# Three quarters of a query projection by Strassen's seven products, in one layer of an encoder

## The chip, the cores and the metric

The kernel runs on one core of one Trainium2 chip. A core has a matrix engine (PE, with its weight loads shown apart as PEld), a vector engine (DVE), an activation engine (ACT), a general engine (POOL) that here mostly issues DMAs, and a queue processor (SP) that only issues DMAs. Each engine runs its own list of instructions in order; they wait for each other by semaphores. The metric is the device time of one execution in microseconds. A lower number is better.

## The reference, cut to what matters

One layer of a streaming encoder on 1024 prompt tokens and 64 decode tokens, model width 1024. The change touches the cross-attention queries and, by a wait, the memory projections.

```python
def memory_kv(mem, norm_mem, w_xk, w_xv, xk_norm):
    mn = rmsnorm(mem, norm_mem)
    mk = rmsnorm((mn @ w_xk).reshape(bsz, N_MEM, N_HEADS_X, HEAD_DIM_X), xk_norm)
    mv = (mn @ w_xv).reshape(bsz, N_MEM, N_HEADS_X, HEAD_DIM_X)
    return mk, mv

def cross_attention(xn, mk, mv, w_xq, xq_norm, w_xo):
    q = rmsnorm((xn @ w_xq).reshape(bsz, t, N_HEADS_X, HEAD_DIM_X), xq_norm)   # 4 heads of 256
    s = jnp.einsum('bqhd,bkhd->bhqk', q, mk).astype(jnp.float32) * (HEAD_DIM_X ** -0.5)
    p = jax.nn.softmax(s, axis=-1).astype(mv.dtype)
    o = jnp.einsum('bhqk,bkhd->bqhd', p, mv).reshape(bsz, t, N_HEADS_X * HEAD_DIM_X)
    return o @ w_xo

def sq_relu_mlp(xn, w_up, w_down):
    return jnp.square(jax.nn.relu(xn @ w_up)) @ w_down
```

## The kernel before

Activations stand transposed: 8 tiles `y(0)` to `y(7)` of 128 features by 1092 token columns (1088 used) in the buffer `Y`. A dense stage is a row of output tiles. For one output tile ("tile" below) a slab of 128x1024 weights is loaded into `RAW`, split by ACT into a high part and by DVE into a low part (`act_split`, `dve_split`), and PE does for each of 8 row blocks the three products high x high, high x low, low x high, each in three column pieces of 364, 364 and 360: 72 matmuls (`pe_part`, L431). The tile builds up in three banks of the eight banks of PE's accumulator memory `ps` and is read out by DVE.

The stages run in the order: memory keys and values (`mem_tile`, 16 tiles of 256 columns), input projection with its mixers, output projection, query projection, cross-attention loop, its output projection, up-projection, down-projection. The up-projection does two tiles densely and the other thirty as 15 pairs by a Strassen scheme: a pair of tiles is a 2x2 block of weights (two output tiles by two halves of the rows) times a 2x2 block of activations (two halves of the rows by two halves of the tokens), which needs 7 products in place of 8. One product is 4 row blocks x 3 terms x 2 pieces of 272 columns = 24 matmuls (`product`, L2950). The combinations of the activation blocks (`t_raw`, `t_hi`, `t_lo`) are made once at the stage's entry, while PE does the two dense tiles; sums of weight blocks (`left_sum`), their split (`left_hi` on ACT, `left_lo` on DVE), copies of products out of `ps` (`prod_copy` on ACT) and the adding up of output blocks (`combine` on DVE) go on beside the products.

The query projection before is eight dense tiles, two for each of four heads. After a head's two tiles its features are squared by ACT (`xq_sq`, L1374), PE adds the squares up (`pe_stat`, L472, 16 matmuls), ACT and DVE turn the sum into a reciprocal root in the row buffer `stat_mix`, PE broadcasts the row in two halves (`pe_bcast`, L484), and DVE scales the head by each half (`xq_nrm`, L2025). A second broadcast waits until DVE has used up the first (semaphore `bc_used`). For head 0 to 2 this stands inside the tiles of the next head, for head 3 inside the attention loop. Before the first head the same is done once for the norm of the input: that broadcast gives `rstd`.

The attention loop has 20 units `u` (5 for each head). For each, PE computes scores of 256 queries by 256 memory rows (`xscores`, L2784, three units ahead), DVE takes the extreme (`xmin`), ACT the exponential (`xexp`), DVE normalises (`xnorm`), PE transposes (`xtransposes`, L2797), ACT and DVE split the transposed weights (`xpt_copy`, `xpt_lo`), and every second unit PE multiplies by the values (`xvalues`, L2817). The values of a head are split at units 0, 1, 4, 11 (ACT L1419, DVE `v_lo`, L2090). Each engine's list is written out by hand; nothing reorders it.

## Time and profile before

| | us |
|---|---|
| time, median of 3 (lowest, highest) | 1517.52 (1516.76, 1517.57) |
| profiled execution: its own time | 1518.14 |
| profiled execution: span | 1516.4 |
| PE busy | 1501.0 |
| DVE busy | 973.0 |
| ACT busy | 585.0 |

The span is what the profiler's instructions cover; 1.7 us of the profiled execution lie around it. Positions below, such as "at 669.75", are microseconds from the start of that span.

### The profile page before, as it was taken

The numbers are of one execution on the slowest core, as the hardware profiler recorded it, in microseconds if no ns is written. First come the engines' busy times: TensorE is split into PE (matmuls) and PEld (weight loads), VectorE is DVE, ScalarE is ACT, GpSimd is POOL, SyncE is SP. The second block draws the span as 40 slices with busy tenths as digits, with TensorE's granted clock in tenths as the row PEclk, the third lists the DMA queues.
The fourth block names the chain that finished last, engine by engine and source line by source line (L and its number), as shares of the span: only waits on it lengthen the run. The fifth ranks groups of instructions, "written<-read, shape, count | busy, mean of one in ns | idle before, by whom it ended". The sixth has DMA issues, their size and how long they took to land.

```text
span 1516.4 us, 26684 instructions
## 1 busy us (share of the span) xinstructions
PE 1501.0 (99%) x10924; PEld 1449.1 (96%) x10924; DVE 973.0 (64%) x1373; ACT 585.0 (39%) x1001; POOL 244.0 (16%) x322
## 2 busy tenths in 40 slices
PE   9999999999999999999999999999999999999999
PEld 8999999988779999997999999999999999999999
DVE  7636787757788443457443986666666597547653
ACT  7521031146675221235323743333434343433332
POOL 1010000002100100000000064445544310010110
PEclk9999999999999999999999999999999999999999
DMA  8425111103112533022222253443345975454663
GB/s 281 144 102 174 54 42 42 46 1 95 70 37 80 167 128 127 15 71 89 71 87 80 79 188 130 160 152 140 136 160 188 322 232 181 120 177 123 187 211 103
DMA packets 64495, 189.33 MB, mean 125 GB/s; under 512 B 7936, under 2 KB 12344, under 8 KB 64240
## 3 DMA queue, kind: packets, MB, share of 16 engines
q1 hardware_dynamic: 39824, 95.30, 19.4%
q0 software_dynamic: 24560, 92.45, 16.9%
q8 instruction: 81, 1.33, 0.4%
q14 instruction: 30, 0.25, 0.1%
HBM read 138.58 MB, written 54.12 MB: 127 GB/s over the span
## 4 chain that ended last, share of the span: by engine, by line
PE 53%; DMA 2%; DVE 1%; issue 0%; ACT 0%; SPq 0%; DVEq 0%; ACTq 0%
PE ps L2950 21%; PE ps L2974 19%; PE ps L431 8%; DMA a<-wdn 2%; PE ps L2784 2%; PE ps L2817 2%; PE ps L2797 0%; DMA r_raw_a<-quads_d 0%; PE ps L2827 0%; DVE Y L2276 0%; PE ps L484 0%; DVE B_lo L2074 0%; PE ps L472 0%; DVE r_lo_a L2251 0%; DVE s L2234 0%
## 5 line engine op out<-in xcount | busy, mean ns | idle before, releaser
L431 PE MATMUL ps<-A_hi,w_hi 128*128 128x364 f32 (+1 forms) x768 | 171.2, 331 | 0.3 <-DVE Y L1640 0.3
L431 PE MATMUL ps<-A_lo,w_hi 128*128 128x364 f32 (+1 forms) x768 | 169.0, 328 | 0.0
L431 PE MATMUL ps<-A_hi,w_lo 128*128 128x364 f32 (+1 forms) x768 | 168.1, 327 | 0.0
L394 ACT ACTIVATE w_hi<-w_raw 128x1024 fp32r<-128x1024 f32 x42 | 44.2, 1058 | 285.8 <-PE ps L431 184.0
L431 PEld LDWEIGHTS ps<-A_hi,w_hi 128*128 128x128 f32 x768 | 130.7, 188 | 7.5 <-issue 6.9
L431 PEld LDWEIGHTS ps<-A_lo,w_hi 128*128 128x128 f32 x768 | 132.7, 188 | 0.0
L431 PEld LDWEIGHTS ps<-A_hi,w_lo 128*128 128x128 f32 x768 | 132.5, 188 | 0.0
L398 DVE TENSOR_TENSOR w_lo<-w_raw,w_hi 128x1024 fp32r<-128x1024 f32 x42 | 51.1, 1222 | 100.5 <-ACT w_hi L394 100.3
L2950 PE MATMUL ps<-t_hi,wq_hi 128*128 128x272 f32 x480 | 99.3, 288 | 0.3 <-issue 0.3
L2950 PE MATMUL ps<-t_lo,wq_hi 128*128 128x272 f32 x480 | 99.2, 288 | 0.0
L2950 PE MATMUL ps<-t_hi,wq_lo 128*128 128x272 f32 x480 | 99.1, 288 | 0.0
L2974 PE MATMUL ps<-r_lo_b,wq_hi 128*128 128x272 f32 x448 | 93.7, 290 | 0.0
L2974 PE MATMUL ps<-r_hi_b,wq_hi 128*128 128x272 f32 x448 | 93.5, 290 | 0.0
L2974 PE MATMUL ps<-r_hi_b,wq_lo 128*128 128x272 f32 x448 | 93.5, 289 | 0.0
L2974 PE MATMUL ps<-r_hi_a,wq_hi 128*128 128x272 f32 x448 | 92.8, 288 | 0.4 <-DVE r_lo_a L2251 0.4
L2974 PE MATMUL ps<-r_lo_a,wq_hi 128*128 128x272 f32 x448 | 92.7, 288 | 0.0
L2974 PE MATMUL ps<-r_hi_a,wq_lo 128*128 128x272 f32 x448 | 92.5, 287 | 0.0
L1700 DVE SCALAR_TENSOR_TENSOR conv_acc<-ua_ext,params,conv_acc 128x1118 f32<-128x1118 f32 x58 | 76.2, 1377 | 0.0
L2950 PEld LDWEIGHTS ps<-t_hi,wq_hi 128*128 128x128 f32 x480 | 75.2, 188 | 0.4 <-issue 0.4
L2950 PEld LDWEIGHTS ps<-t_lo,wq_hi 128*128 128x128 f32 x480 | 75.3, 188 | 0.0
L2950 PEld LDWEIGHTS ps<-t_hi,wq_lo 128*128 128x128 f32 x480 | 75.2, 188 | 0.0
L2950 PE MATMUL ps<-A_hi,wq_lo 128*128 128x272 f32 x360 | 74.5, 288 | 0.0
(334 smaller groups left out, 3560.5 us busy)
## 6 DMA issues: line engine op xcount, KB each, us to landing
w_raw<-slabs SPq DMA_DIRECT2D x67, 512.0 KB, 3.6
quads_d<-quad_sum POOLq DMA_DIRECT2D x64, 272.0 KB, 2.9
w_raw<-wdn POOLq DMA_DIRECT2D x32, 512.0 KB, 3.9
r_raw_a<-quads_d SPq DMA_DIRECT2D x56, 272.0 KB, 3.0
r_raw_b<-quads_d SPq DMA_DIRECT2D x56, 272.0 KB, 3.2
quads_d<-hid_stage POOLq DMA_DIRECT2D x48, 272.0 KB, 3.1
Y<-xT POOLq DMA_DIRECT2D x16, 546.0 KB, 4.9
y_d<-Y POOLq DMA_DIRECT2D x16, 546.0 KB, 3.1
```

What stands on the lines that cost most here:

```text
L394: e.activation(WH[:, par], RAW[:, par], ACT.Copy).then_inc(s.w_hi, 1)
L398: e.tensor_tensor(WL[:, par], RAW[:, par], WH[:, par].bitcast(F32), ALU.subtract).then_inc(s.w_lo, 1)
L431: ins = e.matmul(PS[:, 3 * par + c, 0:n_], wt[:, wpar, w], xt[:, col:col + n_], start=(first and n == 0 and m == 0), stop=(last and n == l ...
L1700: e.scalar_tensor_tensor(CAV[:, h], UE[:, h, j:j + CAW], w, CAV[:, h], ALU.mult, ALU.add)\
L2784: ins = e.matmul(PS[:, u % 3, b * NMEM:(b + 1) * NMEM], y(2 * h + k)[:, q0:q0 + P], XKV[h][:, kk, k * NMEM:(k + 1) * NMEM], start=(k == 0) ...
L2817: ins = e.matmul(PS[:, 6 + d, :], wt[:, h, v0:v0 + P], xt[turn][:, k, :], start=(m == 0 and k == 0), stop=(m == 2 and k == 1))
L2950: ins = e.matmul(PS[:, b + c, 0:HC], WQ[wx][:, n % 4, k * P:(k + 1) * P], right(i, xx, k, c), start=(i in (0, 1, 3) and k == 0 and m == 0) ...
L2974: ins = e.matmul(PS[:, 2 * g + c, 0:HC], WQ[wx][:, down_slot(n), g * P:(g + 1) * P], down_right(xx, n)[:, c * HC:(c + 1) * HC], start=(ii ...
```

## The change

Head 0 keeps its two dense tiles. Heads 1 to 3, six tiles, become three pairs of seven products, with the scheme of the up-projection (`q_product` for `product`, and so on). The block sums of the activations are made at the entry of the query stage in the free buffer `B`, and the blocks of results are put together in `Y`, which is free there once the input has been stored; the scale by `rstd` that was part of reading out a tile is now three extra DVE operations of 128x544 for each pair (`q_scale`) and part of the fourth combine. The squares, statistic, root and broadcasts of each head move: head 0's into the products of pair 1, head 1's into those of pair 2 (in banks 0 and 1), head 2's into the attention loop at units 0 to 2; head 3's stay at units 6 to 11, but their squares move from before the loop to unit 1. The root of heads 0 to 2 is by logarithm and exponential (as head 3's was), so the DVE reciprocal goes. The loads of the heads' keys and values move from the start of the query stage to its last products, since their place holds the activation sums. In the memory stage tiles 6 and 7 wait for the reading of tiles 0 and 1, whose banks they use, where they waited for tiles 4 and 5.

```diff
@@ constants
-S_MEM, S_IN, S_OUT, S_XQ, S_XO, S_UP = 0, 16, 38, 46, 54, 62
+S_MEM, S_IN, S_OUT, S_XQ, S_XO, S_UP = 0, 16, 38, 46, 48, 56
+N_QPAIR = 3
+Q_TURN = [0, 3, 1, 2, 5, 4, 7, 6] + list(range(8, N_QPROD))
@@ SP
+            for p in range(N_QPAIR):
+                if p == 0:
+                    sp.wait_ge(s.w_lo, S_XQ + 2)
+                elif p == 1:
+                    sp.wait_ge(s.t_f, 16)
+                    sp.wait_ge(s.y1_out, 16 * KT)
+                else:
+                    sp.wait_ge(s.sp_lo, 8)
...
-            sp.wait_ge(s.tile_done, S_XQ)
-            for h in range(3):
+            for h, n in enumerate((15, 16, 18)):
+                sp.wait_ge(s.prod, n + 1)
                 load_kv(h)
@@ ACT
+            for q in range(10, N_QPROD):
+                q_copy(Q_TURN[q - 4])
+                q_left_hi(q)
+                if q == 12:
+                    q_root(0)
+                if q == 14:
+                    q_squares(1)
+                if q == 18:
+                    q_root(1, bank=0)
+            q_squares(2)
...
                 xpt_copy(u)
                 if u + 3 < N_XU:
                     xexp(u + 3)
+                if u == 0:
+                    q_root(2)
+                if u == 1:
+                    q_squares(3)
                 if u == X_STAT:
...
                 if u in V_SPLIT:
@@ DVE
+            q_t_raw(0)
+            q_t_raw(1)
+            q_t_lo(0)
             dve_recip(e, cnt)
             cnt.bc += 2
+            q_t_raw(3)
+            q_left_lo(0)
+            q_t_raw(2)
...
+            for q in range(10, N_QPROD):
+                q_combine(Q_TURN[q - 4])
+                if q + 1 < N_QPROD:
+                    q_left_sum(q + 1)
+                q_left_lo(q)
+                q_scale(Q_TURN[q - 4])
+                if q in (13, 19):
+                    q_mix()
+                if q in (14, 15):
+                    xq_nrm(0, q - 14)
+                if q == 20:
+                    xq_nrm(1, 0, lo=0)
...
                 if u in V_SPLIT:
                     v_lo(V_SPLIT[u])
-                if u == X_RECIP:
+                if u in (0, X_RECIP):
+                    q_mix()
+                if u in (1, 2):
+                    xq_nrm(2, u - 1)
@@ PE, memory stage
-            with e.Fori(3, 8) as i:
+            for par in range(2):
+                e.wait_ge(s.w_lo, 7 + par)
+                e.wait_ge(s.tile_read, 1 + par)
+                mem_tile(par)
+            with e.Fori(4, 8) as i:
@@ PE, query stage
-            for h in range(3):
-                xq_tile(2 * h + 2)
-                xq_stat(h)
...
-            tile_part(7, range(4))
-            pe_bcast(e, cnt, 0, rc_wait(n_rc))
-            tile_part(7, (4,))
-            pe_bcast(e, cnt, 1)
-            e.wait_ge(s.tile_read, S_XO - 1)
-            xscores(0)
-            tile_part(7, (5,))
-            xscores(1)
-            tile_part(7, (6,))
-            xscores(2)
-            tile_part(7, (7,))
+            for n, q in enumerate(Q_TURN):
+                q_product(q)
+                if n == 8:
+                    e.wait_ge(s.u_rel, 4)
+                    xq_stat(0)
+                    n_rc += 1
+                if n in (10, 11):
+                    pe_bcast(e, cnt, n - 10, rc_wait(n_rc))
+                if n == 14:
+                    e.wait_ge(s.u_rel, 8)
+                    xq_stat(1, bank=0)
+                    n_rc += 1
+                if n in (16, 17):
+                    pe_bcast(e, cnt, n - 16, rc_wait(n_rc), lo=0)
+                if n == 18:
+                    e.wait_ge(s.bc_used, cnt.used(cnt.bc))
+                    xscores(0)
+                if n == 19:
+                    xscores(1)
+            e.wait_ge(s.u_add, 3 * N_QPAIR)
             xscores(2)
@@ PE, attention loop (u)
                 xtransposes(u)
...
+                if u == 0:
+                    e.wait_ge(s.u_rel, 4 * N_QPAIR)
+                    xq_stat(2)
+                    n_rc += 1
+                if u in (1, 2):
+                    pe_bcast(e, cnt, u - 1, rc_wait(n_rc))
```

The two DVE steps of a pair that are new against a dense tile:

```python
            def q_combine(q):

                p, i = divmod(q, 7)
                if i < 3:
                    return
                e.wait_ge(s.prod, Q_POS[q] + 1)
                e.wait_ge(s.y1_out, 16 * KT)
                if p:
                    e.wait_ge(s.stat_done, N_STAT_X + p)
                if i < 6:
                    t = {3: 0, 4: 1, 5: 2}[i]
                    e.wait_ge(s.p_copy, 3 * p + t + 1)
                    e.tensor_tensor(halves(q_quad(p, i)), ps_pair(bank(p, i)), halves(QTMP[t][:, :]), ALU.add)\
                        .then_inc(s.u_add, 1)
                else:
                    e.tensor_tensor(halves(q_quad(p, i)), ps_pair(bank(p, i)), halves(RSTD[:, 0:HT]), ALU.mult)\
                        .then_inc(s.u_rel, 1)

            def q_scale(q):

                p, i = divmod(q, 7)
                if i not in (3, 4, 5):
                    return
                n = QUAD[i][1]
                e.wait_ge(s.u_add, 3 * p + i - 2)
                e.tensor_tensor(q_quad(p, i), q_quad(p, i), RSTD[:, n * HT:(n + 1) * HT], ALU.mult).then_inc(s.u_rel, 1)
```

The order moves at three places. The first is the entry of the query stage on DVE. Before, after the last low part of the weights, comes the row for the first broadcast:

```order
L2002 TENSOR_TENSOR rstd<-rstd,square 128x1092 [waits acc_done,sq_done]
L398 TENSOR_TENSOR w_lo<-w_raw,w_hi 128x1024 [waits w_hi]
L519 RECIPROCAL stat_row<-stat_row 128x273 [waits stat_read]
L523 TENSOR_SCALAR stat_mix<-stat_row,row_mask 128x273 [waits sel_ready,rc_step]
L525 SCALAR_TENSOR_TENSOR stat_mix<-stat_row,row_mask,stat_mix 128x273 [waits rc_step]
L398 TENSOR_TENSOR w_lo<-w_raw,w_hi 128x1024 [waits w_hi,bc_used]
```

Now (`xt_raw` and `xt_lo` are the block sums of the activations and their low parts):

```order
L2128 TENSOR_TENSOR rstd<-rstd,square 128x1092 [waits acc_done,sq_done]
L412 TENSOR_TENSOR w_lo<-w_raw,w_hi 128x1024 [waits w_hi]
L2163 SCALAR_TENSOR_TENSOR xt_raw<-Y,params,x_scaled 128x544 [waits t_x] x4
L2163 SCALAR_TENSOR_TENSOR xt_raw<-Y,params,xt_raw 128x544 [waits t_f] x4
L2168 TENSOR_TENSOR xt_lo<-xt_raw,xt_hi 128x544 [waits t_hi] x4
L533 RECIPROCAL stat_row<-stat_row 128x273 [waits stat_read]
L537 TENSOR_SCALAR stat_mix<-stat_row,row_mask 128x273 [waits sel_ready,rc_step]
L539 SCALAR_TENSOR_TENSOR stat_mix<-stat_row,row_mask,stat_mix 128x273 [waits rc_step]
L2163 SCALAR_TENSOR_TENSOR xt_raw<-Y,params,xt_raw 128x544 [waits t_f] x4
L2194 TENSOR_TENSOR wq_lo<-w_raw,wq_hi 128x512 [waits sp_hi]
```

Twelve operations of 128x544 now stand between the last `w_lo` and the row `stat_mix`, which PE's first broadcast waits for.

The second place is the start of the attention loop on PE, from the scores of unit 3 on. Before:

```order
L2784 MATMUL ps<-xkv_124,Y 128x256 [waits x_exp,bc_used]
L2797 MATMUL ps<-ident,x_scores 128x128 [waits x_p,tile_read]
L2784 MATMUL ps<-xkv_124,Y 128x256 [waits x_exp,bc_used]
L2797 MATMUL ps<-ident,x_scores 128x128 [waits x_p]
L2784 MATMUL ps<-xkv_125,Y 128x256 [waits x_exp,xkv_in1,bc_used]
L2797 MATMUL ps<-ident,x_scores 128x128 [waits x_p]
L2784 MATMUL ps<-xkv_125,Y 128x256 [waits x_exp,bc_used]
L2797 MATMUL ps<-ident,x_scores 128x128 [waits x_plo,x_pt,x_p]
L2817 MATMUL ps<-xpt_hi_128,xv_hi 128x512 [waits x_plo,stat_read,x_vlo,bc_used,x_pt]
```

Now, with the statistic of head 2 (L486) and its two broadcasts (L498) between the same rows:

```order
L3087 MATMUL ps<-xkv_124,Y 128x256 [waits x_exp,bc_used]
L3100 MATMUL ps<-ident,x_scores 128x128 [waits x_p]
L486 MATMUL ps<-xq_sq_122,ones 32x273 [waits stat_read,bc_used,xs_sq,u_rel]
L3087 MATMUL ps<-xkv_124,Y 128x256 [waits x_exp,bc_used]
L3100 MATMUL ps<-ident,x_scores 128x128 [waits x_p]
L498 MATMUL ps<-stat_mix,row_sel 128x274 [waits bc_used,rc_done]
L3087 MATMUL ps<-xkv_125,Y 128x256 [waits x_exp,xkv_in1,bc_used]
L3100 MATMUL ps<-ident,x_scores 128x128 [waits x_p]
L498 MATMUL ps<-stat_mix,row_sel 128x274 [waits bc_used,rc_done]
L3087 MATMUL ps<-xkv_125,Y 128x256 [waits x_exp,bc_used]
L3100 MATMUL ps<-ident,x_scores 128x128 [waits x_plo,x_pt,x_p]
L3120 MATMUL ps<-xpt_hi_128,xv_hi 128x512 [waits x_plo,stat_read,x_vlo,bc_used,x_pt]
```

PE meets the first broadcast after one unit's transposes, the second one unit later, and the first values (the last row) wait for both to be used.

The third is the same stretch on ACT and DVE. ACT before, from the squares of head 3 on:

```order
L1374 ACTIVATE xq_sq_122<-Y 128x1092 [waits stat_done,tile_read]
L1374 ACTIVATE xq_sq_123<-Y 128x1092 [waits stat_done,tile_read]
L1390 ACTIVATE xpt_hi_128<-ps 128x2x256 [waits x_t]
L1357 ACTIVATE x_scores,exp_sum<-ps,neg_max 128x256 [waits x_rec,x_t,x_min]
L1357 ACTIVATE x_scores,exp_sum<-ps,neg_max 128x256
L1419 ACTIVATE xv_hi<-xkv_124 128x512 [waits tile_done,xkv_in0]
L1390 ACTIVATE xpt_hi_128<-ps 128x2x256 [waits x_t]
L1357 ACTIVATE x_scores,exp_sum<-ps,neg_max 128x256 [waits x_rec,x_t,x_min]
L1419 ACTIVATE xv_hi<-xkv_125 128x512 [waits tile_done,xkv_in1]
```

ACT now:

```order
L1518 ACTIVATE xpt_hi_128<-ps 128x2x256 [waits x_t]
L1501 ACTIVATE x_scores,exp_sum<-ps,neg_max 128x256 [waits x_rec,x_t,x_min]
L1501 ACTIVATE x_scores,exp_sum<-ps,neg_max 128x256
L1454 ACTIVATE stat_row<-ps,eps 128x273 [waits bc_done,stat_done]
L1456 ACTIVATE stat_row<-stat_row 128x273 [waits x_ln]
L1545 ACTIVATE xv_hi<-xkv_124 128x512 [waits prod,xkv_in0]
L1518 ACTIVATE xpt_hi_128<-ps 128x2x256 [waits x_t]
L1501 ACTIVATE x_scores,exp_sum<-ps,neg_max 128x256 [waits x_rec,x_t,x_min]
L1449 ACTIVATE xq_sq_122<-Y 128x1092 [waits stat_done,u_rel]
L1449 ACTIVATE xq_sq_123<-Y 128x1092
L1545 ACTIVATE xv_hi<-xkv_125 128x512 [waits prod,xkv_in1]
```

The squares (L1449) stand behind the exponential of unit 4 and ahead of the value split of head 1 (the last row); the root of head 2 (L1454, L1456) stands ahead of the value split of head 0. DVE now, in that stretch (before, it had neither the mix L537 and L539 nor L2238 here):

```order
L2341 TENSOR_TENSOR xpt_lo_131<-ps,xpt_hi_128 128x2x256 [waits x_pt]
L2346 TENSOR_TENSOR xv_lo<-xkv_124,xv_hi 128x512 [waits x_vhi]
L537 TENSOR_SCALAR stat_mix<-stat_row,row_mask 128x273 [waits sel_ready,stat_read]
L539 SCALAR_TENSOR_TENSOR stat_mix<-stat_row,row_mask,stat_mix 128x273 [waits rc_step]
L2249 TENSOR_REDUCE neg_max<-ps 128x1 [waits x_exp,x_s]
L2258 RECIPROCAL exp_rec<-exp_sum 128x2 [waits x_p,x_exp]
L2260 TENSOR_TENSOR x_scores<-x_scores,exp_rec 128x512 [waits x_rec]
L2341 TENSOR_TENSOR xpt_lo_131<-ps,xpt_hi_128 128x2x256 [waits x_pt]
L2346 TENSOR_TENSOR xv_lo<-xkv_125,xv_hi 128x512 [waits x_vhi]
L2238 SCALAR_TENSOR_TENSOR Y<-Y,gq_scaled,ps 128x546 [waits u_rel,bc_done,xs_sq]
L2238 SCALAR_TENSOR_TENSOR Y<-Y,gq_scaled,ps 128x546
```

The scaling by the first broadcast of head 2 (L2238) stands behind the low part of head 1's values (`xv_lo<-xkv_125`).

## Rows read from the trace of the kernel before

**Rows 1.** Page, part 1: busy time of each engine.

```profile
PE 1501.0 (99%) x10924; PEld 1449.1 (96%) x10924; DVE 973.0 (64%) x1373; ACT 585.0 (39%) x1001; POOL 244.0 (16%) x322
```

**Rows 2.** Stretch 677:740: its us, busy us (instructions) of PE, PEld, DVE, ACT, POOL.

```profile
677.00:740.00 63.00, 59.95 (x333) 51.10 (x332) 45.42 (x90) 34.09 (x96) 3.70 (x7) 1.00 0.29 92
```

**Rows 3.** Chain of waits, in order of time: start us, us, what.

```profile
739.49 102.81 PE ps L431 x621
...
855.72 21.28 PE ps L2950 x168
...
877.26 295.42 PE ps L2950 x2352
```

**Rows 4.** DVE in order of time, entry of the up-projection: start us, us, what.

```profile
836.91 1.22 DVE L398 TENSOR_TENSOR w_lo<-w_raw,w_hi 128x1024 fp32r<-128x1024 f32 x1
...
843.61 2.63 DVE L2160 TENSOR_TENSOR t_lo<-t_raw,t_hi 128x544 fp32r<-128x544 f32 x4
846.15 1.86 DVE L519 RECIPROCAL stat_row<-stat_row 128x273 f32<-128x273 f32 x1
...
848.45 0.51 DVE L525 SCALAR_TENSOR_TENSOR stat_mix<-stat_row,row_mask,stat_mix 128x273 fp32r<-128x273 f32 x1
```

**Rows 5.** DVE in order of time, entry of the query projection.

```profile
568.86 1.22 DVE L398 TENSOR_TENSOR w_lo<-w_raw,w_hi 128x1024 fp32r<-128x1024 f32 x1
...
577.73 0.50 DVE L525 SCALAR_TENSOR_TENSOR stat_mix<-stat_row,row_mask,stat_mix 128x273 fp32r<-128x273 f32 x1
```

**Rows 6.** PE in order of time, first broadcast of the query stage.

```profile
579.35 0.42 PE L484 MATMUL ps<-stat_mix,row_sel 128*128 128x274 f32 x2
```

**Rows 7.** Single lines of DVE: duration ns min/median/max, first and last start us.

```profile
L2195 DVE TENSOR_TENSOR wq_lo<-w_sum,wq_hi x60: 678/693/1857, 859.9 to 1158.8; 128x512 fp32r<-128x512 f32 x60
...
L2025 DVE SCALAR_TENSOR_TENSOR Y<-Y,gq_scaled,ps x16: 774/778/784, 607.0 to 713.0; 128x546 f32<-128x546 f32 x16
```

**Rows 8.** Chain of waits, first turns of the attention loop.

```profile
669.75 1.73 PE ps L2784 x8
671.48 0.44 PE ps L2797 x4
...
677.55 2.79 PE ps L2817 x12
...
690.10 1.13 PE ps L472 x16
```

**Rows 9.** ACT in order of time, attention loop.

```profile
669.94 2.29 ACT L1374 ACTIVATE xq_sq<-Y 128x1092 f32<-128x1092 f32 x2
...
673.51 0.63 ACT L1419 ACTIVATE xv_hi<-xkv 128x512 fp32r<-128x512 f32 x1
...
691.29 0.49 ACT L1410 ACTIVATE stat_row<-ps,eps 128x273 f32<-128x273 f32 x1 [0.32 <-PE ps L472]
```

**Rows 10.** SP in order of time: first load of keys and values before.

```profile
562.40 0.40 SPq L801 DMA_DIRECT2D xkv<-o_mk  x1
562.85 0.46 SPq L801 DMA_DIRECT2D xkv<-o_mv  x1
```

**Rows 11.** DMA issues: KB each, median us from issue to landing.

```profile
xkv<-mvc SPq DMA_DIRECT2D x4, 256.0 KB, 5.8
```

**Rows 12.** Memory stage: DVE, then PE, in order of time.

```profile
27.26 1.22 DVE L408 TENSOR_TENSOR w_lo<-w_raw_mem,w_hi 128x1024 fp32r<-128x1024 f32 x1
...
28.87 0.38 PE L2358 MATMUL ps<-mem_hi,w_hi 128*128 128x256 f32 x1 [0.92 <-DVE mem_kv L1597]
```

**Rows 13.** PE in order of time, start of the kernel.

```profile
6.41 0.41 PE L2358 MATMUL ps<-mem_hi,w_lo 128*128 128x256 f32 x1
6.62 0.41 PE L2358 MATMUL ps<-mem_hi,w_hi 128*128 128x256 f32 x1
...
7.94 0.28 PE L2358 MATMUL ps<-mem_lo,w_hi 128*128 128x256 f32 x1
8.06 0.29 PE L2358 MATMUL ps<-mem_hi,w_lo 128*128 128x256 f32 x1
```

More of the change, by code:

```diff
@@ L1027, in _ @@
                 quads(hp)
[L1028 removed]
+            g.wait_ge(s.sp_lo, Q_PROD + N_PROD)
             stream_load(g, 0)
@@ L1346, in _, with q_scaled, q_t_hi @@
                     residual(S_OUT, i, par, "norm_x", 8)
+            def q_scaled(i):
+                if i == 1:
+                    e.wait_ge(s.tile_done, S_XQ)
+                    e.wait_ge(s.tile_read, S_XQ)
+                lo = 0 if i == 1 else HT
+                for k in range(4):
+                    e.activation(XTX[i][:, k], y(k)[:, lo:lo + HT], ACT.Copy, scale=par_col("norm_x", k)).then_inc(s.t_x, 1)
+            def q_t_hi(i):
+                for k in range(4):
+                    e.wait_ge(s.t_f, 16 if i == 3 else 4 * T_RAW.index(i) + k + 1)
+                    e.activation(XTH[i][:, k], XTF[i][:, k], ACT.Copy).then_inc(s.t_hi, 1)
@@ new lines, in q_squares @@
+            def q_squares(h):
+                if h == 0:
+                    e.wait_ge(s.tile_read, S_XQ + 2)
+                    e.wait_ge(s.t_f, 16)
+                    e.wait_ge(s.y1_out, 16 * KT)
+                else:
+                    e.wait_ge(s.u_rel, 4 * h)
+                    if h == 1:
+                        e.wait_ge(s.sp_lo, 14)
+                    elif h == 2:
+                        e.wait_ge(s.prod, 16)
+                    else:
+                        e.wait_ge(s.stat_done, N_STAT_X + 3)
+                for k in range(2):
+                    e.activation(q_square(h, k), y(2 * h + k), ACT.Square).then_inc(s.xs_sq, 1)
@@ L2053, in _ @@
+            q_t_raw(2)
             e.wait_ge(s.bc_used, cnt.used(cnt.bc))
[L2054 to L2067 removed]
+            xevac(0)
@@ new lines, in _ @@
+            q_left_lo(3)
+            xevac(1)
+            q_left_sum(1)
+            q_left_sum(2)
+            q_left_lo(1)
+            q_t_lo(1)
+            q_left_lo(2)
+            q_left_sum(5)
+            q_left_sum(4)
+            q_left_lo(5)
+            q_left_lo(4)
+            q_t_lo(2)
+            q_left_lo(7)
+            q_t_lo(3)
+            q_left_lo(6)
+            q_combine(3)
+            q_combine(4)
+            q_left_sum(8)
+            q_left_lo(8)
+            q_combine(5)
```

388 lines of the change are left out of this document (278 added, 110 removed).

## The prediction

> **What bounds the kernel now.** I read the busy times first: PE works 1501.0 of 1516.4 us, DVE 973.0, ACT 585.0 [rows 1]. The end can move only with PE's list: by the work in it and by the holes in it. The chain of waits then gives the price of that work where PE goes without a break: 621 matmuls of a dense tile in 102.81 us, 0.1656 us each, and 2352 matmuls of Strassen products in 295.42 us, 0.1256 us each [rows 3]. In the attention loop PE is busy 59.95 of 63.00 us, so the holes there are 3.05 us in all [rows 2]; from the start of the query stage at about 562 to 677 it has none. So whatever the new order makes PE wait for is a loss in full, and I looked for the places where the others' lists, now longer, are late.
>
> **What goes.** Six dense tiles are 6 x 72 = 432 matmuls, 71.5 us. Three pairs are 3 x 168 = 504 matmuls of 0.1256, 63.3 us; the first pair of the up-projection, where PE changes over, took 21.28 for 168 [rows 3], which would be 63.8. Gain 8.2 to 7.7; I take 8.0. Statistics, broadcasts, scores and transposes are as many as before.
>
> In the memory stage PE stood 0.92 us at 28.87 for the reading of an earlier tile [rows 12]. The new wait drops that, and next late is the weight split that ends at 27.26 + 1.22 = 28.48, so PE can start at about 28.54: 0.3 less. The tile after it meets a split as tightly, so between 0 and 0.35; I take 0.3.
>
> **What comes, place by place.** *Entry of the query stage.* DVE has twelve operations of 128x544 between the last `w_lo` and the broadcast row. The up-projection has the same twelve in the same place: from the start of its `w_lo` at 836.91 to the end of the row at 848.45 + 0.51 = 848.96 are 12.05 us, of which DVE idles nothing [rows 4]. From the query stage's `w_lo` at 568.86 [rows 5] that gives 580.91 for the row that was ready at 578.23. PE comes to it at 579.35 [rows 6], after three of eight row blocks (the up-projection's list has four ahead). Wait: 580.91 + 0.1 - 579.35 = 1.65 us. The bounds are 1.3 and 2.0, by a few tenths of slack in either list.
>
> *Steady products.* A product lasts 24 x 0.1256 = 3.01 us. For each pair DVE has 4 sums and 7 low parts of 512 columns, 4 combines and 3 scalings of 544. One of 512 lasts 0.69 [rows 7], but neighbours overlap: four of 544 take 846.15 - 843.61 = 2.54, so 0.63 each [rows 4], and I take 0.60 for 512. That is 11.0 us of 21.1, so DVE has room, and the up-projection runs 14 pairs so, with more DVE work, without a hole. I count no wait but at the broadcasts, as these have two operations of 0.78 [rows 7] behind the others. With E as the end of product 10 (where the first broadcast of head 0 goes): DVE gets the product about 0.2 later, combines 0.63, sums 0.60, low part 0.60, scales 0.63, and only then scales the head, 1.48: ready at 4.15. PE is back after the broadcast 0.35 and one product 3.01, at 3.36. Wait 0.8. For head 1 there is no combine, sum or scaling ahead: ACT copies the third product (0.5) and makes the high part (0.5), DVE the low part, then 1.48: ready about 3.45 against 3.36, wait 0.1 to 0.2. The mixes before these broadcasts end 2.9 after a product whose successor ends at 3.01: no wait, with 0.1 of slack. Together 1.0, with bounds 0.3 and 2.0.
>
> *Start of the attention loop.* This is the largest term. Let 0 be the end of the last product. PE has scores 2 and 3 (1.73 each), transposes (0.44), the statistic (1.13), the half-size scores of unit 4 (0.87) and transposes again [rows 8]: it comes to the first broadcast of head 2 at 6.3. DVE: extreme of unit 3 from 3.5, normalising of unit 2 (0.8 with its reciprocal) and low part to 5.5. ACT: copy of the transposes at 4.1, two exponentials to 5.5, root 0.95 to 6.4, and only behind it the split of head 0's values [rows 9], whose low part on DVE starts 0.67 later, at 7.1; the mix follows, 0.9, and the row is ready at 8.6. Wait 2.4. PE then broadcasts 0.35, scores 1.73, transposes 0.44: at the second broadcast at 11.2. It needs DVE to have used the first. DVE stands behind the low part of head 1's values, that behind the ACT split of them, and this behind both squares of head 3, 2.2 us [rows 9], which ACT starts at 9.5, after the exponential of unit 4. So the split starts at 11.7, its low part at 12.4, the scaling at 13.0 and ends at 14.4. Wait 3.3. Last, the first values wait until the second broadcast is used: DVE reaches that after extreme, normalising and low part at 16.0 and ends at 17.5; PE is there at 17.0. Wait 0.5. Sum 6.2. In the loop before, the same PE rows from 669.75 to 677.55 had no hole [rows 8], because the roots and squares of head 2 lay in the tiles ahead. Could the lists be kinder? At best DVE finds the value split early and only one of the waits stays: 2.5. At worst exponentials and copies each slip by one place: 9. From the first values on, DVE's place against PE is what it was before, so I carry nothing further, and the 3.05 of holes stay.
>
> The late load of the values costs nothing: SP issues the first after product 15, about 9.7 us ahead of scores 0 (products 16 to 18 and the broadcasts between), where the old one went at 562.40, 97 us ahead. The four parts go out 0.45 to 0.5 apart [rows 10], and the slowest kind lands 5.8 after its issue [rows 11]: 2 + 5.8 = 7.8, so 1.9 is left.
>
> **Sum.** -8.0 - 0.3 + 1.65 + 1.0 + 6.2 = +0.55. The profiled execution took 1518.14 (span 1516.4 and 1.7 around it), so 1518.7; it stands 0.6 above the median of 1517.52, so against the median 1518.1. The terms' bounds add up to -4.2 and +5.
>
> **A rule on the clock.** PE's matmuls of 256 columns follow each other by 0.21 us at 6.41 and by 0.12 at 7.94 [rows 13]: the lower and the higher of its two clocks (1.2 and 2.4 GHz). It had been working since 1.55. Later no such pitch appears [rows 3], but the loop's holes before are 3.05 us spread over 63 [rows 2], and my loop start has 2.4 and 3.3 within 8 us. If the clock fell there, and a stretch as at the start (1.55 to 7.6, 6 us) ran at half speed, 3 us of work would be lost; that is the upper end, nothing the lower. The Trainium skill ("TensorE: Matmul & The Clock Gate", section "HAM oscillation — how this bites in real kernels") states that waits between bursts of matmuls bring the half clock back. By that rule the sum would be 1521.1; by the rows, which have no such fall, 1518.1.
>
> **The rivals.**
> - *A: gain and waits about cancel* (the forecast), 1518.1; its own range is 1515 to 1521. For it: the same twelve operations in the up-projection, and an ACT list whose order is fixed. Against: small errors in four queues add up. Chance 0.57.
> - *B: the waits are not there*, and the pairs give what they save: -8.3, 1509.2; with the entry wait alone 1510.9. For it: the up-projection runs 15 pairs with one hole, 0.26 at 877.00 [rows 3]. Against: it has no attention loop behind it and no heads' norms within. Halfway, at 1513 to 1514, is a loop start in which ACT's squares come early. Chance 0.20.
> - *C: the clock falls in the holes at the loop's start.* Place: PE's rows after the first broadcasts of head 2; price up to 3; it decides once a hole is long enough, which the trace does not show. 1521.1, slower. Chance 0.15.
> - *D: the values come too late.* The XKV loads wait behind product 15 and PE stands at scores 0. The load must take over 9.7 us, 1.9 more than worked out above; each microsecond beyond counts. With 13 us, 1521.4. Chance 0.08.
>
> **How the numbers follow.** About 0.2%, 3 us, is what a measurement of this kernel can tell from no change. A gives same 0.44, slower 0.08, faster 0.05; B faster 0.17, same 0.03; C slower 0.10, same 0.05; D slower 0.06, same 0.02. Together faster 0.22, same 0.54, slower 0.24. The range for 8 in 10 reaches into B's halfway case and covers C: 1512.5 to 1521.8.
>
> **What would show it.** PE's matmuls of the products at 0.126 from start to start, 504 of them in about 63.5 us. PE idle before the first broadcast of the query stage 1.6 us, released by the DVE row; before the second broadcast of head 0 about 0.8; in the first three units of the loop about 2.4, 3.3 and 0.5, the middle one with ACT's squares in front. PE's busy time down by about 8 us, its idle time up by about 8 or 9. I am wrong if the loop start shows no hole over 1 us (then B), if matmuls behind a hole follow at twice their pitch (C), or if scores 0 wait for a DMA (D).

## The result, and the profile after

The changed kernel takes 1519.58 us (median of 20 runs, 1518.07 to 1522.00), the kernel before 1517.59 beside it (20 runs, 1516.76 to 1519.30): the ratio is 1.0013, with the interval 1.0007 to 1.0018. That is 2.0 us longer, and within the 0.2% that I called no change. The forecast was 1518.1. The profiled execution has a span of 1518.3 us, 1.9 more than before.

Busy time of each engine (the page after; before it is [rows 1]):

```profile
PE 1495.1 (98%) x10996; PEld 1442.3 (95%) x10996; DVE 1008.5 (66%) x1444; ACT 612.4 (40%) x1052; POOL 244.3 (16%) x322
```

PE works 5.9 us less (1501.0 to 1495.1) and the kernel is 1.9 longer, so PE's idle time grew by 7.8. Where it stands idle, all of PE's timeline from the query stage to the first values shows (start us, busy us, instruction, and in brackets the idle time before it and what ended it):

```profile
580.53 0.52 PE L498 MATMUL ps<-stat_mix,row_sel 128*128 128x274 f32 x2 [1.44 <-DVE stat_mix L539]
...
616.08 1.13 PE L486 MATMUL ps<-Y,ones 128*32 128x273 f32 x16 [0.21 <-DVE Y L2212]
...
627.58 0.49 PE L498 MATMUL ps<-stat_mix,row_sel 128*128 128x274 f32 x2 [0.86 <-DVE Y L2238]
...
669.17 0.52 PE L498 MATMUL ps<-stat_mix,row_sel 128*128 128x274 f32 x2 [1.95 <-DVE stat_mix L539]
669.53 1.89 PE L3087 MATMUL ps<-xkv,Y 128*128 128x256 f32 x8
...
674.84 0.49 PE L498 MATMUL ps<-stat_mix,row_sel 128*128 128x274 f32 x2 [2.98 <-DVE Y L2238]
675.16 2.97 PE L3087 MATMUL ps<-xkv,Y 128*128 128x256 f32 x8
```

Four of the holes are where the prediction had them: at the entry, at head 0's second broadcast and twice at the loop's start. The one of 0.21, before the statistic of head 0, it did not have. The last row holds the surprise: the same eight score matmuls that take 1.89 behind the hole of 1.95 take 2.97 behind the hole of 2.98. The granted clock says why. Two stretches of the kernel after (length, busy us and instructions of PE, PEld, DVE, ACT, POOL, then PE's granted clock):

```profile
669.00:675.00 6.00, 2.85 (x15) 2.38 (x16) 4.21 (x9) 3.58 (x6) 0.54 (x1) 1.00 0.44 140
675.30:679.00 3.70, 3.70 (x14) 3.07 (x13) 3.27 (x8) 1.02 (x4) 0.00 (x0) 0.57 0.11 46
```

In the first PE is half idle and its clock is whole. In the second it is always busy and the clock is 0.57, so for most of the stretch it is at the lower of the two levels, 1.2 GHz. Transfers are no explanation: the share of the DMA engines (the last figure but one) is 0.44 in the first stretch and 0.11 in the second.

The fall is not peculiar to the profiled execution. Each execution reports the mean granted clock of its whole run, and one stretch like this lowers it by 0.001. All 20 executions of the changed kernel have 0.997 to 0.999 there. Of the 72 executions of the kernel before that the runs below were measured beside, 69 have 1.000; the other three, with 0.998 or 0.999, take 1520.87 to 1522.45.

The chain of waits over this place (start us, us, what):

```profile
668.22 0.37 DVE stat_mix L537
...
669.86 0.19 ACT x_scores L1501
670.05 1.89 ACT xq_sq L1449 x2
671.94 0.03 issue
671.96 0.62 ACT xv_hi L1545
...
673.22 1.48 DVE Y L2238 x2
674.70 0.14 issue
674.84 0.49 PE ps L498 x2
675.33 2.80 PE ps L3087 x8
678.13 0.85 PE ps L3100 x4
678.98 2.97 PE ps L3120 x12
```

It runs in the order that was worked out: squares of head 3, split of head 1's values, low part, scaling, second broadcast. Then come 2.80 + 0.85 for what took 1.73 + 0.44 in [rows 8]: 1.48 us lost to the clock. The first values start at 678.98 where they started at 677.55.

### The profile page after: what moved, and what is told of

The parts are those of the page before. It is cut to its first block, busy times and chain, and to the rows that moved or that the text cites. A ratio compares the mean times of both kernels' runs of the same rounds, so it can differ in the third digit from the quotient of the medians.

```text
span 1518.3 us, 26980 instructions
## 1 busy us (share of the span) xinstructions
PE 1495.1 (98%) x10996; PEld 1442.3 (95%) x10996; DVE 1008.5 (66%) x1444; ACT 612.4 (40%) x1052; POOL 244.3 (16%) x322
## 4 chain that ended last, share of the span: by engine, by line
PE 85%; DVE 6%; DMA 4%; ACT 2%; issue 2%; SPq 0%; DVEq 0%; ACTq 0%
PE ps L445 29%; PE ps L3267 20%; PE ps L3291 19%; PE ps L3070 3%; DMA a<-wdn 3%; PE ps L2614 2%; PE ps L2863 2%; PE ps L3087 2%; PE ps L2914 2%; PE ps L3120 2%; PE ps L2888 2%; DVE t_raw L2411 1%; PE ps L486 1%; DVE pt L2035 0%; DVE B_lo L2047 0%
## 5 line engine op out<-in xcount | busy, mean ns | idle before, releaser
L445 PE MATMUL ps<-A_hi,w_hi 128*128 128x364 f32 (+1 forms) x624 | 138.7, 330 | 0.3 <-DVE Y L1766 0.3
L445 PE MATMUL ps<-A_lo,w_hi 128*128 128x364 f32 (+1 forms) x624 | 137.3, 328 | 0.0
L445 PE MATMUL ps<-A_hi,w_lo 128*128 128x364 f32 (+1 forms) x624 | 136.7, 327 | 0.0
L408 ACT ACTIVATE w_hi<-w_raw 128x1024 fp32r<-128x1024 f32 x36 | 37.9, 1060 | 242.3 <-PE ps L445 140.8
L445 PEld LDWEIGHTS ps<-A_hi,w_hi 128*128 128x128 f32 x624 | 106.1, 188 | 6.1 <-issue 5.6
L445 PEld LDWEIGHTS ps<-A_lo,w_hi 128*128 128x128 f32 x624 | 107.8, 188 | 0.0
L445 PEld LDWEIGHTS ps<-A_hi,w_lo 128*128 128x128 f32 x624 | 107.7, 188 | 0.0
L3291 PE MATMUL ps<-r_lo_b,wq_hi 128*128 128x272 f32 x448 | 93.6, 290 | 0.0
L3291 PE MATMUL ps<-r_hi_b,wq_hi 128*128 128x272 f32 x448 | 93.5, 290 | 0.0
L3291 PE MATMUL ps<-r_hi_b,wq_lo 128*128 128x272 f32 x448 | 93.5, 289 | 0.0
L3291 PE MATMUL ps<-r_hi_a,wq_hi 128*128 128x272 f32 x448 | 92.8, 288 | 0.6 <-DVE r_lo_a L2507 0.6
L3291 PE MATMUL ps<-r_lo_a,wq_hi 128*128 128x272 f32 x448 | 92.6, 288 | 0.0
L3291 PE MATMUL ps<-r_hi_a,wq_lo 128*128 128x272 f32 x448 | 92.5, 287 | 0.0
L412 DVE TENSOR_TENSOR w_lo<-w_raw,w_hi 128x1024 fp32r<-128x1024 f32 x36 | 43.8, 1222 | 68.4 <-ACT w_hi L408 68.2
L3267 PE MATMUL ps<-A_hi,wq_hi 128*128 128x272 f32 x360 | 74.3, 288 | 0.3 <-DVE hid_stage L2390 0.3
```

The source lines that it names most:

```text
L408: e.activation(WH[:, par], RAW[:, par], ACT.Copy).then_inc(s.w_hi, 1)
L412: e.tensor_tensor(WL[:, par], RAW[:, par], WH[:, par].bitcast(F32), ALU.subtract).then_inc(s.w_lo, 1)
L445: ins = e.matmul(PS[:, 3 * par + c, 0:n_], wt[:, wpar, w], xt[:, col:col + n_], start=(first and n == 0 and m == 0), stop=(last and n == l ...
L3267: ins = e.matmul(PS[:, b + c, 0:HC], WQ[wx][:, n % 4, k * P:(k + 1) * P], right(i, xx, k, c), start=(i in (0, 1, 3) and k == 0 and m == 0) ...
L3291: ins = e.matmul(PS[:, 2 * g + c, 0:HC], WQ[wx][:, down_slot(n), g * P:(g + 1) * P], down_right(xx, n)[:, c * HC:(c + 1) * HC], start=(ii ...
```

## The experiments

How soon the first stages are done differs by up to 1.7 us between the profiled executions (560.47 to 562.16 for the same matmul), so beside the medians I use one length within the trace: from the first matmul of query tile 0 to the matmul behind the loop that waits for ACT's `x_scores`. In the kernel after that is this row:

```profile
729.27 0.76 PE L445 MATMUL ps<-B_hi,w_hi_b 128*128 128x364 f32 x3 [1.20 <-ACT x_scores L1501]
```

The length is 165.48 us before (562.16 to 727.64) and 167.53 after (561.74 to 729.27): +2.05, as much as the whole difference. I call it the stage.

**The changed kernel again (a2_changed_again).** No edit.

> The changed kernel once more, beside the others. If the low clock behind a hole depends on when the hole falls and not only on its length, its profile will show the fall behind the first hole of the loop (1.95 us) in some executions and behind the second (2.98) in others; the order of work fixes the holes, so they stay at these lengths or, behind an early fall, the second is shorter by what the slow matmuls took. Time 1.9 to 2.0 over the kernel before. Rival (a fixed rule of length alone): the fall always behind the second.

Measured 1519.90 (1519.32 to 1522.41, 11 runs), ratio to before 1.0018 (1.0009 to 1.0027); stage 167.48. PE at the loop's start:

```profile
674.52 0.70 PE L498 MATMUL ps<-stat_mix,row_sel 128*128 128x274 f32 x2 [2.98 <-DVE Y L2238]
675.02 3.38 PE L3087 MATMUL ps<-xkv,Y 128*128 128x256 f32 x8
```

The same hole, and the lower clock behind it a second time: the broadcast takes 0.70 for 0.49 and the scores 3.38 for 1.89. Here the broadcast itself is slow already, which it was not in the first profile, so the fall does not come at a fixed distance from the hole. All 11 executions have a granted clock below 1.000. Both profiles have the fall behind the second hole, so this run alone could not tell a rule of length from one of moment; the next two runs do.

**Head 3's squares two units later (e1_squares_unit3).** This takes away what ACT had ahead of the split of head 1's values in the second hole.

```diff
-                if u == 1:
+                if u == 3:
                     q_squares(3)
```

> The changed kernel with one step moved: ACT squares head 3 in unit 3 of the attention loop, not in unit 1. My theory (holes on PE, and a lower clock behind the long one): the hole of 2.98 us before the second broadcast of head 2 shrinks to about 0.9, since the value split no longer stands behind the squares; with so short a hole the clock is granted in full behind it, which gives back 1.5 more; a hole of up to 0.5 before the first values may appear. In all 3.0 less than the changed kernel, about 1516.6, 1.0 under the kernel before. Rival (the slow matmuls at 675 are from transfers into SBUF at that time, not from the clock): 2.1 less, about 1517.5, and the eight scores behind the broadcast still take 2.8 us.

Measured 1517.21 (1516.44 to 1521.12, 11 runs), ratio 0.9998 (0.9989 to 1.0007). PE:

```profile
669.55 0.52 PE L498 MATMUL ps<-stat_mix,row_sel 128*128 128x274 f32 x2 [1.95 <-DVE stat_mix L539]
669.91 3.22 PE L3087 MATMUL ps<-xkv,Y 128*128 128x256 f32 x8
...
673.63 0.54 PE L498 MATMUL ps<-stat_mix,row_sel 128*128 128x274 f32 x2
674.01 1.89 PE L3087 MATMUL ps<-xkv,Y 128*128 128x256 f32 x8
...
676.76 0.70 PE L3120 MATMUL ps<-xpt_hi,xv_hi 128*128 128x512 f32 x2 [0.43 <-issue]
```

The second hole is gone, but not by the squares alone. DVE's scaling shows their share:

```profile
671.74 1.47 DVE L2238 SCALAR_TENSOR_TENSOR Y<-Y,gq_scaled,ps 128x546 f32<-128x546 f32 x2
```

It ends 3.7 us after the start of the first broadcast (669.55), where in the changed kernel it ended 5.5 after (674.70 against 669.17): 1.9 of the 2.98 are the squares'. The other 1.1 are hidden, because PE itself comes 1.4 later: the scores behind the *first* hole are slow, 3.22 for 1.89. So neither expectation came true as a whole: the hole behaves as I thought, but the clock is not granted in full. A hole of 1.95 can also bring the lower clock, though the same hole did not in the two profiles above. The rival, transfers at about 675, is out: the scores behind the second broadcast are back at 1.89. And the third hole, 0.43, appears, the one that I had predicted as 0.5. The stage is 164.99, 2.5 shorter than in the changed kernel: 2.98 won, 0.43 given back, and the clock paid once in either kernel. (Of the 11 executions three have a granted clock of 1.000; they take 1517.18 to 1517.22.)

**The root ahead of the low part (e2_root_first).** At the entry of the query stage.

```diff
             q_t_raw(1)
-            q_t_lo(0)
             dve_recip(e, cnt)
             cnt.bc += 2
+            q_t_lo(0)
             q_t_raw(3)
```

> The changed kernel with DVE's reciprocal and mix of the input norm ahead of the four low parts of the first block sum, not behind them. My theory: the row is ready at 578.4, before PE comes to its first broadcast, so the hole of 1.44 us goes and nothing later is late, as the low parts are first read by product 2 at about 595: 1.4 less than the changed kernel, 1518.2. Rival (DVE's list is full up to the first products, so that the wait moves to product 0 or 1): no change, 1519.6.

Measured 1517.56 (1516.65 to 1518.76, 11 runs), ratio 0.9997 (0.9989 to 1.0006); stage 165.02. The hole of 1.44 is gone and no product of the first pair is late. The loop's start:

```profile
666.79 0.52 PE L498 MATMUL ps<-stat_mix,row_sel 128*128 128x274 f32 x2 [1.95 <-DVE stat_mix L539]
667.15 2.92 PE L3087 MATMUL ps<-xkv,Y 128*128 128x256 f32 x8
669.86 1.06 PE L3100 MATMUL ps<-ident,x_scores 128*128 128x128 f32 x4
672.45 0.49 PE L498 MATMUL ps<-stat_mix,row_sel 128*128 128x274 f32 x2 [1.53 <-DVE Y L2238]
```

Here too the clock falls behind the hole of 1.95. The scores are 1.0 longer and the transposes 0.5, and since PE comes 1.45 later to the second broadcast, which has not moved, its hole is 1.53 in place of 2.98. So slow matmuls ahead of a hole cost nothing, and behind the last hole they cost in full. Behind 1.53 the scores take 1.89 as always. In numbers: 1.44 from the entry and 1.49 from the clock are won, 0.42 comes as the third hole, 2.5 in all, as the stage shows. By my expectation only the 1.44 would have gone; the other microsecond is the clock, which fell where its cost is hidden. The squares stand where they stood, and 1.53 of the hole is left here where none is in e1, which is the second sign that they are a part of it.

**Work in the hole (e3_fill_hole).** PE gets 25 matmuls to do before the second broadcast, into a free bank; nothing reads them.

```diff
+                if u == 2:
+                    e.wait_ge(s.x_vhi, 1)
+                    e.wait_ge(s.x_exp, xexps(4))
+                    for _ in range(25):
+                        e.matmul(PS[:, 0, 0:208], XV[0][:, 0, 0:P], XV[0][:, 0, 0:208], start=True, stop=True)
                 if u in (1, 2):
                     pe_bcast(e, cnt, u - 1, rc_wait(n_rc))
```

> The changed kernel with 25 extra matmuls of 208 columns, whose results nobody reads, on PE just before the second broadcast of head 2, where it stood idle 2.98 us; they take about 2.4 us. My theory (the clock fell because PE stood still there): the clock stays in full, the scores behind take 1.73 us and not 2.80, and the time falls by 1.0 to 1.5 us although PE has more to do: 1518.1 to 1518.6. Rival (transfers or readers of the same memory slow these matmuls): scores still at 2.80, time unchanged at 1519.6 or up to 0.5 more.

Measured 1518.52 (1517.88 to 1525.15, 12 runs), ratio 1.0012 (1.0001 to 1.0022). PE, and below it the clock:

```profile
670.36 3.02 PE L3175 MATMUL ps<-xv_hi 128*128 128x208 f32 x25
673.58 0.49 PE L498 MATMUL ps<-stat_mix,row_sel 128*128 128x274 f32 x2 [0.20 <-DVE Y L2238]
673.90 1.89 PE L3087 MATMUL ps<-xkv,Y 128*128 128x256 f32 x8
```

```profile
664.00:680.00 16.00, 13.44 (x86) 11.20 (x77) 11.40 (x22) 9.29 (x25) 1.07 (x2) 1.00 0.40 145
```

The broadcast waits for the same DVE row and is no earlier, but PE had work meanwhile; the clock stays whole and the scores take 1.89. The stage is 166.50, 1.0 shorter than in the changed kernel, though it does 25 matmuls more: 1.5 is won from the clock, and the third hole comes back with 0.42. That the emptiness of the hole lowers the clock is shown by this pair, and what it costs: 1.5 us of slow matmuls, 1.0 net, since they had covered the third hole. The medians agree (1.1 less), but their intervals overlap.

**Long holes and short ones in the kernel before (h4_long_holes, h1_short_holes).** Both put five waits on PE behind query tiles 2 to 6 for the reading of the tile just done; in the second the reading comes first on DVE, so that the wait is short.

```diff
@@ both: PE
             def xq_stat(h):
+                if h < 3:
+                    e.wait_ge(s.tile_read, S_XQ + 2 * h + 3)
...
                     norm_tile(i)
+                    e.wait_ge(s.tile_read, S_XQ + i + 1)
@@ h1_short_holes alone: DVE
                 if i < 6:
+                    xevac(i)
                     dve_split(e, S_XQ + i + 2, i % 2)
...
-                xevac(i)
+                if i >= 6:
+                    xevac(i)
```

> The kernel before with five holes made on PE in the dense query stage: behind tiles 2 to 6 PE waits until DVE has read that tile out, which here comes behind a weight split on ACT and one on DVE, so each hole is about 3.8 us. My theory: each hole costs its length and behind it the matmuls follow at half pace (0.33 in place of 0.166 from start to start) for a stretch, at a cost of 1 to 3 us each: 5 x (3.8 + 1.5) = 26 more than before, 1544. Rival (no fall of the clock from such holes in dense work): 5 x 3.8 = 19 more, 1537.

> The kernel before with the same five waits behind tiles 2 to 6 as in the run with long holes, but DVE reads the tile out ahead of its weight split, so each hole is about 1.4 us where it was 3.67. My theory: no fall of the clock behind any of them, as behind the single one of 1.39 there; five holes of 1.4 cost 7.0: 1524.6. Rival (a short hole lowers the clock too, now and then): 1526 or more, and the matmuls behind some holes at 0.30 from start to start.

One execution each: 1543.11 with the long holes, 1525.04 with the short, both within 1 us of what was expected with the fall and without it. The kernel before has 1517.53 and 1517.66 on the same two chips. PE's waits, first long, then short (us in total, times, longest):

```profile
PE ps L472 <- DVE Y L2017: 8.7, 3, 3.7
PE ps L431 <- DVE Y L2017: 7.3, 2, 3.7
```

```profile
PE ps L472 <- DVE Y L2017: 4.2, 3, 1.4
PE ps L431 <- DVE Y L2017: 2.8, 2, 1.4
```

Four holes of 3.67 and one of 1.39 against five of 1.39. Idle time alone makes 16.0 - 7.0 = 9.0 of the 18.1 us between them; the rest is 9.1 for the four long holes. Its place behind the first of them:

```profile
602.74 2.05 PE L472 MATMUL ps<-xq_sq,ones 128*32 128x273 f32 x16 [3.67 <-DVE Y L2017]
...
605.79 1.11 PE L431 MATMUL ps<-A_lo,w_hi 128*128 128x364 f32 x3
...
609.72 0.66 PE L431 MATMUL ps<-A_hi,w_hi 128*128 128x364 f32 x3
```

```profile
602.80:609.00 6.20, 6.20 (x30) 4.81 (x31) 2.73 (x3) 0.49 (x1) 0.00 (x0) 0.50 0.21 78
609.00:613.00 4.00, 4.00 (x27) 4.00 (x26) 0.00 (x0) 0.00 (x0) 0.00 (x0) 1.00 0.00 0
```

Behind 3.67 us of nothing, in a stretch that is dense on both sides, PE runs at exactly half clock for about 6 us, then at the whole. Behind the second hole it takes only half as long:

```profile
622.97 1.27 PE L431 MATMUL ps<-A_hi,w_hi 128*128 128x364 f32 x3 [3.67 <-DVE Y L2017]
624.95 1.11 PE L431 MATMUL ps<-A_hi,w_lo 128*128 128x364 f32 x3
626.43 0.65 PE L431 MATMUL ps<-A_lo,w_hi 128*128 128x364 f32 x3
```

The third hole goes like the first (slow until 646.7, 6.5 behind its end) and the fourth like the second (until 663.6, 3.1). Half of such a stretch is lost, so two of the four holes cost about 3.1 beyond their length and two about 1.5: together about 9.2, against the 9.1 that are to be explained. With the short holes the clock is 1.00 from 562 to 680. The matmuls are the kernel's own and the same in both, so the clock hangs on the hole and not on anything in the change.

**The memory wait alone (e4_mem_wait_alone).** The kernel before with the two waits of the memory stage.

> The kernel before with only the new waits of memory tiles 6 and 7. My theory: PE starts tile 6 0.36 to 0.42 us earlier and nothing gives it back before the end: 0.4 less than before, about 1517.2. Rival (DVE or a transfer in the mixers sets the pace later): no change.

Measured 1518.57 (1517.19 to 1523.74, 12 runs), ratio 1.0009 (0.9999 to 1.0019), which decides nothing about 0.3 us. The trace does. In both kernels PE's wait at tile 6 has the length and the releaser that this row of the changed one shows (0.55 in e4):

```profile
28.45 0.38 PE L2614 MATMUL ps<-mem_hi,w_hi 128*128 128x256 f32 x1 [0.56 <-DVE w_lo L422]
```

The wait is now for `w_lo`, and from the start of tile 5 to that of tile 6 are 3.67 us in e4 and 3.66 in the changed kernel, 4.01 before: 0.34 to 0.35 less, as predicted.

**A rearranged loop start (b2_rearranged, b3_split_later, b5_squares_unit2).** All three have the root first, the norms of a head at the front of DVE's turn, and head 2's root and statistic moved ahead of the loop; the split of head 1's values is two units later than in the changed kernel, that of head 2's and the first values one unit.

```diff
@@ DVE, products
+                if q in (14, 15):
+                    xq_nrm(0, q - 14)
+                if q == 20:
+                    xq_nrm(1, 0, lo=0)
                 q_combine(Q_TURN[q - 4])
...
-                if q in (14, 15):
-                    xq_nrm(0, q - 14)
-                if q == 20:
-                    xq_nrm(1, 0, lo=0)
@@ ACT: q_root(2) behind the first three xexp, squares later
-                if u == 0:
-                    q_root(2)
-                if u == 1:
+                if u == 3:
                     q_squares(3)
@@ PE: statistic of head 2 behind scores 2, before the loop
             xscores(2)
+            e.wait_ge(s.u_rel, 4 * N_QPAIR)
+            xq_stat(2)
+            n_rc += 1
@@ DVE, loop: mix at u == 0 and first norm at u == 1 behind xmin, second norm at u == 2 behind xpt_lo
@@ plan
-        X_VALUES = {3: 0, 5: 1, ...
-        V_SPLIT = {0: 0, 1: 1, 4: 2, 11: 3}
+        X_VALUES = {4: 0, 5: 1, ...
+        V_SPLIT = {0: 0, 3: 1, 5: 2, 11: 3}
@@ b3_split_later against b2_rearranged
-        V_SPLIT = {0: 0, 3: 1, 5: 2, 11: 3}
+        V_SPLIT = {2: 0, 3: 1, 5: 2, 11: 3}
@@ b5_squares_unit2 against b2_rearranged
-                if u == 3:
+                if u == 2:
                     q_squares(3)
```

> The changed kernel with its holes taken away by order alone: DVE's reciprocal first at the entry; the scalings of heads 0 and 1 by a broadcast ahead of the combine and split of the same turn; head 2's statistic on PE ahead of scores 3, its root on ACT ahead of the loop, its mix and scalings earlier on DVE; the squares of head 3 in unit 3; the value split of head 1 in unit 3 and of head 2 in unit 5; the first values of head 0 in unit 4. My theory: holes of 1.44, 0.86 and 0.12 go, the 1.95 becomes 0.1, the 2.98 about 1.35, and the clock stays in full, so 1.5 more comes back: about 1512.1, 5.5 under the kernel before. Rival (the gain of the products is smaller than 8 us, as the changed kernel only shows 7.2 of work less): 1513.0. Rival 2 (the shorter holes still lower the clock): 1513.6.

Measured 1514.24 (1513.12 to 1516.57, 11 runs), ratio 0.9980 (0.9971 to 0.9989); stage 163.09. PE, then ACT, then the stretch behind the second hole:

```profile
667.69 0.49 PE L498 MATMUL ps<-stat_mix,row_sel 128*128 128x274 f32 x2 [1.12 <-DVE Y L2237]
...
680.52 1.19 PE L3123 MATMUL ps<-xpt_hi,xv_hi 128*128 128x512 f32 x2 [2.34 <-ACT xpt_hi L1519]
```

```profile
673.60 2.11 ACT L1449 ACTIVATE xq_sq<-Y 128x1092 f32<-128x1092 f32 x2
```

```profile
680.50:684.00 3.50, 3.48 (x10) 2.79 (x11) 2.77 (x6) 1.70 (x6) 0.00 (x0) 0.59 0.00 0
```

Of the old holes 1.12 is left, but the squares, moved to unit 3, now make the copy of the transposes late in front of the second values: 2.34, with the clock at 0.59 behind it. So the time is 2.1 over the 1512.1 that I expected. This run also shows the price of the fall between executions of one kernel. Six of the 11 have a granted clock of 1.000 and take 1513.12 to 1514.24; the five with 0.999 take 1515.33 to 1516.57. The same list of work has the fall or not, and it costs 1.9 us between the medians of the two groups.

> As the rearranged kernel, with head 0's value split in unit 2 as well. My theory: DVE reaches the first scaling of head 2 by 0.6 us earlier, so the hole before the second broadcast is 0.75 and the time 0.6 less, 1511.5. Rival (the split is then late for the first values in unit 4): the same or up to 0.5 more.

Measured 1515.33 (1513.73 to 1518.51, 11 runs), ratio 0.9986 (0.9977 to 0.9995), stage again 163.09. The broadcast's hole goes down to 0.52, and the first values get one of 0.51:

```profile
672.31 0.70 PE L3123 MATMUL ps<-xpt_hi,xv_hi 128*128 128x512 f32 x2 [0.51 <-DVE xv_lo L2345]
```

What one place won the next gave back; I had expected 0.6 less. The hole before the second values is 2.30 here, with the fall behind it. The median is 1.1 over that of the run before because more of the executions have the fall: eight of 11 are below 1.000, and the other three take 1513.73 to 1514.28.

> The rearranged kernel (first values of head 0 in unit 4) with the squares of head 3 in unit 2 instead of unit 3. In the rearranged kernel these squares (2.11 us on ACT from 673.60) pushed the exponential of unit 7, the high part of the first values and the copy behind them, and PE stood 2.34 us before the second values, with the clock low behind it. ACT is idle for 1.6 to 2.3 us just before, so here the squares fit there. My theory: the hole before the second values shrinks to 0.9 or less and the clock stays in full: 2.4 less than the rearranged kernel, 1511.8. Rival (the second values wait for the split of the first values anyway, which begins only when these are done): the hole stays over 1.5, 1513.5.

Measured 1512.57 (1511.92 to 1512.97, 6 runs) against 1517.66 before (10 runs), ratio 0.9967 (0.9955 to 0.9979); stage 160.06. PE:

```profile
668.18 0.49 PE L498 MATMUL ps<-stat_mix,row_sel 128*128 128x274 f32 x2 [1.13 <-DVE Y L2237]
...
679.30 0.70 PE L3123 MATMUL ps<-xpt_hi,xv_hi 128*128 128x512 f32 x2 [0.63 <-ACT xpt_hi L1519]
```

No hole up to the second values is over 1.13, the granted clock from 560 to 742 is 1.00 (and 1.000 in all six executions), and this version beats both kernels, by 5 us the one before and, by the two ratios, by 7 the changed one. The hole came out as 0.63 where 0.9 or less was expected. The kernel before has no wait over 0.2 us from query tile 0 to the second values, and behind them its holes are the ones that stand here too (0.71, 1.07 and 1.20), so the order could win nothing in it and what is won belongs to the Strassen pairs: the work saved was there all along, and the order of the other engines' lists, and the clock, had taken it away.

## Why the prediction came out so, step by step

- *The gain of 8.0.* A product's matmul was taken as 0.1256. The chain of the changed kernel has

```profile
588.76 18.11 PE ps L3070 x144
```

  0.1258 each, so the price holds. But from query tile 0 to the first values there are 117.24 us (561.74 to 678.98) against 115.39 before. Less the holes (1.44 + 0.21 + 0.86 + 0.12 + 1.95 + 2.98 = 7.56) and the 1.48 of the clock, 108.2 us of work are left: 7.2 less than before, not 8.0. The products are not what is missing. Counted from start to start of PE's rows, the eight dense tiles took 96.9 us; now the two tiles take 24.2 and the products 64.5, together 8.2 less. The missing 1.0 lies around them, in good part at the holes: the transposes ahead of the two long ones hold PE 0.60 where they held it 0.43 before, and broadcasts behind a hole take 0.49 to 0.52 where [rows 6] has 0.42. So the price of a matmul was right, and a hole costs a few tenths more than its length.
- *Memory, 0.3.* 0.34, released by `w_lo` as said.
- *Entry, 1.65.* 1.44, released by the row that was named; e2 took away what stood ahead of it, and the hole went.
- *Broadcasts of heads 0 and 1, 1.0.* 0.86 at the second of head 0 (0.8 was forecast) and 0.12 at that of head 1. The mixes made no wait, as said, but the statistic ahead of the first of them waited 0.21, for which the prediction has no term. In all 1.2.
- *Loop start, 6.2.* The holes are 1.95, 2.98 and none, 4.9 in all, for 2.4, 3.3 and 0.5. The order of events was right at each: squares on ACT from 669.95, 9.2 behind the last product where 9.5 was forecast; split from 671.96, 11.2 where 11.7 was. The third hole was not absent: slow matmuls lay over it, and with the clock whole it is there (0.43, 0.42, 0.42 in e1, e2, e3).
- *The clock.* This is the step that failed, though the time came out near. I wrote that "by the rows, which have no such fall", the sum stays at 1518.1, and gave the fall a chance of 0.15 by itself. It came in both profiles of the changed kernel and, by the mean granted clock, in all of its 31 executions. It cost 1.5 of the 3 that I had as its upper end, 1.0 net (e3). It is also why PE's busy time fell by 5.9 and not by the 8 that I named as a sign: the 1.5 of slow matmuls count as busy. The rows of before could not show it, since none of the 3.05 us of holes in its loop [rows 2] is over 1.2; I took the absence of a fall there as a reason against one. The Trainium skill ("TensorE: Matmul & The Clock Gate", section "HAM oscillation — how this bites in real kernels") says that waits between bursts of matmuls bring the half clock back, and the trace agrees: 0.57 behind 2.98, 0.50 behind 3.67.
- *The values' load (rival D).* Not late. The load is issued at 641.43 and scores 0 start at 651.14 without a wait, 9.7 later as worked out.

(The bounds of the terms, "-4.2 and +5", hold the gain at 8.0; with its own 7.7 to 8.2 they are -4.5 and +5.3. Nothing else hangs on it.)

Summed anew: -7.2 - 0.34 + 1.44 + 1.19 + 4.93 + 1.48 = +1.5, where +0.55 was forecast and +1.9 to +2.0 measured. Of the remaining 0.4, 0.2 is at L3291 in the up-projection (a wait of 0.6 for 0.4). So the forecast was near partly by luck. Cases A and C came together: a clock that was left out (1.5) and costs around the holes that were left out (0.8) were for the most part made up for by holes at the loop's start that were 1.3 shorter than worked out. The mechanism, a gain about cancelled by waits at named places, was right. Rival B was wrong as a forecast, but it tells what the pairs are worth: with most of the waits taken out the kernel stands at 1512.57.

## What to carry to other kernels

When the busiest engine is given less to do, write down the lists of the engines that serve it over that stretch and time each release against its arrival: the five waits that showed in the changed kernel where one was forecast were each within half a microsecond, and the sixth lay under slow matmuls. Price a hole of TensorE like the ones here, of about 2 us and more, not by its length alone but also by the slower matmuls behind it, and first break the longest one up, by moving the instruction that stands ahead of its releaser. When such an instruction is moved, look for what it is then ahead of: the squares at unit 1 made 1.9 of a hole of 2.98 at a broadcast, at unit 3 of the rearranged loop they made one of 2.34 at the second values, and at unit 2 only 0.63 there.
